# Two rows of gains: folded into scaled rows, or held as columns and applied where turned rows are split

## The chip, the cores and the metric

The kernel runs on one core of a Trainium2 chip. Its time is device microseconds for one execution; several executions give a median. Engines are named as the profile names them: PE (matrix multiplication, and transposition through the same array), DVE (vector), ACT (scalar activations), POOL, and SP, whose only work here is to issue transfers.

## What is computed

Two blocks of a sequence model on 256 tokens of width 2048, all in float32. The part that matters here is the middle of the second block: the residual `x` is normalised once for keys and values, and once for queries, with two different rows of gains (2048 numbers each).

```python
def rmsnorm(x, g):
    xf = x.astype(jnp.float32)
    inv = lax.rsqrt(jnp.mean(xf * xf, axis=-1, keepdims=True) + RMS_EPS)
    return (xf * inv).astype(x.dtype) * g
...
            x = x + (y * jax.nn.silu(gate)) @ w_out_a[i]
            if layer == N_A_LAYERS - 1:
                kv_in = rmsnorm(x, norm_kv)
                k_shared = apply_rope((kv_in @ w_k).reshape(b, s, HEADS_PER_GROUP, HEAD_DIM), cos, sin)
                v_shared = (kv_in @ w_v).reshape(b, s, HEADS_PER_GROUP, HEAD_DIM)
        else:
            i = layer - N_A_LAYERS
            hdn = rmsnorm(x, norm_b[i])
            proj = hdn @ w_in_b[i]
```

Nothing changes `x` between the two normalisations, so both use the same inverse root of the mean square, and only the gains differ.

## The kernel before

Every matrix product is done with three products of rounded parts: a weight tile is split into a high part (ACT, line 852) and the rest, the low part (DVE, line 1275), and activations likewise (`x_high` on ACT, line 879; `x_low` on DVE, line 1299). Weights flow through in units of 0.5 MB (128 partitions x 1024 numbers) in one fixed order: SP loads unit n into one of 4 raw slots once the low part of unit n-4 is made; the split parts sit in 8 slots, so ACT makes the high part of unit n+8 only when PE has used unit n. `freed(n)` in the ACT and DVE programs does that step, and before it one step of whatever stands `aside`. Each engine runs its own program in written order; semaphores tie them together.

The tokens are two halves of 128. A `wide` job computes a 256x512 piece of a product, with 16 tiles of 128 rows of weights, in 8 units of two tiles; for each unit it does half 0, then half 1, three 128x512 matmuls a tile. `wide_by_half` does half 0 over all 8 units and then half 1, so that the rows of half 0 are complete early. The order around the change is: the last pair of gate and group jobs of the pooling layer, four wide jobs `proj_a` (w_out_a; they add to the residual, line 1675), four wide jobs `vals` (w_v), the keys (w_k), then queries with attention.

A row of activations has to be turned (transposed) before it can be the operand that carries the contraction over partitions. `turned` in the PE program (line 652) turns 128x128 tiles against an identity matrix into PSUM (`aux_banks`, 4 banks of 512 columns, so one piece of 4 tiles to a bank, 4 pieces to a half); ACT and DVE then split a piece into `act_a` (keys and values) or `act_b` (queries). DVE first makes the scaled rows, with `rstd` (one number for a token) and the row of gains in one operation (`scale_rows`, line 1315, for keys; line 1709 for queries). The gains are loaded by `load_row` as one row repeated over all partitions, 1 MB each, after the weight units up to the third unit of the second projection job.

## Time and profile before

| | |
|---|---|
| median of 3 runs | 2030.54 us (2030.03 to 2031.4) |
| the profiled execution's own time | 2030.97 us |
| its span, first to last instruction | 2028.8 us |
| PE busy | 2005.8 us (99%) |
| DVE, ACT busy | 1408.6 us (69%), 1010.2 us (50%) |
| mean granted clock | 0.999 |

The span is what the rows below are read against; 2.2 us of the execution lie outside of it. Busy time of PE is the union of its matmuls, so 99% says that it hardly ever stood still, and not how well each matmul was used.

### The profile page before, as it was taken

How to read it: one execution, taken by the hardware profiler on the slowest of the kernel's cores; microseconds unless marked ns; L12 is line 12 of the kernel's file. 1: busy time of each engine (PE TensorE's matmuls, PEld its weight loads, DVE VectorE, ACT ScalarE, POOL GpSimd, SP SyncE). 2: the span in 40 equal slices, each digit the busy share in tenths (PEclk: the TensorE clock that was granted, in tenths of full speed). 3: DMA queues.
4: the chain of work that ended last, by engine and by line, in shares of the span. 5: the costliest groups of instructions: out<-in, count | busy, mean ns of one | idle time of the engine just before them, and what ended most of it. 6: DMA issues, size and time to landing. Idle time of an engine off the chain costs nothing.

```text
span 2028.8 us, 28149 instructions
## 1 busy us (share of the span) xinstructions
PE 2005.8 (99%) x11404; PEld 1759.0 (87%) x11404; DVE 1408.6 (69%) x1722; ACT 1010.2 (50%) x1340; POOL 8.0 (0%) x19
## 2 busy tenths in 40 slices
PE   7999999999999999999999999999999999999998
PEld 7999988888888888888888898888888888888887
DVE  6999967665555555565577766566577888888764
ACT  5767555544444444444455455445444545454543
POOL 0000000000000000000000000000000000000000
PEclk9999999999999999999999999999999999999999
DMA  8655564866656566665637665656565454545573
GB/s 272 187 181 171 182 223 133 275 218 187 196 184 199 186 190 197 186 198 187 195 96 230 188 215 193 227 187 214 187 193 182 151 171 150 173 154 178 171 264 105
DMA packets 305857, 384.24 MB, mean 189 GB/s; under 512 B 11673, under 2 KB 237209, under 8 KB 303936
## 3 DMA queue, kind: packets, MB, share of 16 engines
q1 hardware_dynamic: 305584, 382.38, 59.6%
q8 instruction: 90, 1.47, 0.3%
q14 instruction: 39, 0.32, 0.0%
q10 hardware_dynamic: 144, 0.07, 0.0%
HBM read 378.20 MB, written 4.19 MB: 188 GB/s over the span
## 4 chain that ended last, share of the span: by engine, by line
PE 96%; DMA 1%; DVE 1%; issue 1%; ACT 1%; SPq 0%; POOL 0%; ACTq 0%; POOLq 0%; DVEq 0%
PE job_banks L545 32%; PE job_banks L548 16%; PE job_banks L617 11%; PE job_banks L615 11%; PE job_banks L616 11%; PE job_banks L517 3%; PE job_banks L516 3%; PE job_banks L518 3%; PE aux_banks L787 2%; DMA raw_weights<-in_w_up 1%; PE aux_banks L652 1%; DMA resid<-in_x 1%; PE aux_banks L518 0%; PE aux_banks L517 0%; PE aux_banks L516 0%
## 5 line engine op out<-in xcount | busy, mean ns | idle before, releaser
L1275 DVE TENSOR_TENSOR weights_low<-raw_weights,weights_high 128x1024 fp32r<-128x1024 f32 x696 | 841.8, 1223 | 473.9 <-ACT weights_high L852 468.8
L852 ACT ACTIVATE weights_high<-raw_weights 128x1024 fp32r<-128x1024 f32 x696 | 728.0, 1056 | 605.8 <-PE job_banks L617 243.2
L545 PE MATMUL job_banks<-act_a,weights_high 128*128 128x512 f32 (+1 forms) x2008 | 590.3, 380 | 5.9 <-DVE act_a L1299 4.5
L548 PEld LDWEIGHTS job_banks<-act_a,weights_low 128*128 128x128 f32 x1880 | 347.5, 188 | 75.6
L548 PE MATMUL job_banks<-act_a,weights_low 128*128 128x256 f32 (+1 forms) x1880 | 368.7, 277 | 0.0
L545 PE MATMUL job_banks<-act_b,weights_high 128*128 128x512 f32 x1024 | 326.9, 400 | 0.0
L545 PEld LDWEIGHTS job_banks<-act_a,weights_high 128*128 128x128 f32 x2008 | 303.7, 190 | 7.5 <-issue 5.0
L615 PE MATMUL job_banks<-weights_high,act_b 128*128 128x512 f32 x736 | 287.1, 390 | 0.0
L617 PE MATMUL job_banks<-weights_high,act_b 128*128 128x512 f32 x736 | 286.4, 389 | 0.0
L616 PE MATMUL job_banks<-weights_low,act_b 128*128 128x512 f32 x736 | 286.4, 389 | 0.0
L548 PEld LDWEIGHTS job_banks<-act_b,weights_low 128*128 128x128 f32 x1024 | 192.3, 188 | 45.1
L548 PE MATMUL job_banks<-act_b,weights_low 128*128 128x256 f32 x1024 | 201.5, 278 | 0.0
L516 PE MATMUL job_banks<-act_a,weights_high 128*128 128x256 f32 x576 | 163.2, 283 | 0.0
L617 PEld LDWEIGHTS job_banks<-weights_high,act_b 128*128 128x128 f32 x736 | 138.1, 188 | 28.7
L517 PE MATMUL job_banks<-act_a,weights_high 128*128 128x256 f32 x576 | 163.0, 283 | 0.0
L518 PE MATMUL job_banks<-act_a,weights_low 128*128 128x256 f32 x576 | 163.0, 283 | 0.0
L615 PEld LDWEIGHTS job_banks<-weights_high,act_b 128*128 128x128 f32 x736 | 138.2, 188 | 28.2
L616 PEld LDWEIGHTS job_banks<-weights_low,act_b 128*128 128x128 f32 x736 | 138.2, 188 | 28.2
L545 PEld LDWEIGHTS job_banks<-act_b,weights_high 128*128 128x128 f32 x1024 | 157.2, 189 | 0.8
L517 PEld LDWEIGHTS job_banks<-act_a,weights_high 128*128 128x128 f32 x576 | 110.6, 192 | 0.0
L516 PEld LDWEIGHTS job_banks<-act_a,weights_high 128*128 128x128 f32 x576 | 110.6, 192 | 0.0
L518 PEld LDWEIGHTS job_banks<-act_a,weights_low 128*128 128x128 f32 x576 | 110.6, 192 | 0.0
(146 smaller groups left out, 1683.3 us busy)
## 6 DMA issues: line engine op xcount, KB each, us to landing
raw_weights<-in_w_up SPq DMA_DIRECT2D x128, 512.0 KB, 3.8
raw_weights<-in_w_down SPq DMA_DIRECT2D x128, 512.0 KB, 4.3
raw_weights<-in_w_in_b SPq DMA_DIRECT2D x128, 512.0 KB, 4.1
raw_weights<-in_w_in SPq DMA_DIRECT2D x80, 512.0 KB, 3.9
raw_weights<-in_w_in_a SPq DMA_DIRECT2D x64, 512.0 KB, 4.7
raw_weights<-in_w_out SPq DMA_DIRECT2D x32, 512.0 KB, 4.4
raw_weights<-in_w_out_a SPq DMA_DIRECT2D x32, 512.0 KB, 4.4
raw_weights<-in_w_v SPq DMA_DIRECT2D x32, 512.0 KB, 4.4
```

The source lines that it names most:

```text
L516: e.matmul(o[:, f, :], wh[:, k, cols], xh, start=kt == 0 and f == 0, stop=False)
L517: e.matmul(o[:, f, :], wh[:, k, cols], xl, start=False, stop=False)
L518: made = e.matmul(o[:, f, :], wl[:, k, cols], xh, start=False, stop=kt == job.tiles - 1 and f == 1)
L545: made = e.matmul(o_both, wh[:, k, f * P:(f + 1) * P], rhs, start=opens, stop=False)
L548: made = e.matmul(o[:, 0, low_toks], wl[:, k, f * P:(f + 1) * P], x[:, first + kt, 0, low_toks], start=False, stop=kt == job.tiles - 1)
L615: e.matmul(o, xh, wh[:, k, :], start=opens and kt == 0, stop=False)
L616: e.matmul(o, xh, wl[:, k, :], start=False, stop=False)
L617: made = e.matmul(o, xl, wh[:, k, :], start=False, stop=closes and kt == job.tiles - 1)
L652: made = e.transpose(aux[:, c, i * P:(i + 1) * P], n[:, k * P:(k + 1) * P], ident[:, :])
L787: made = e.matmul(scores_of(half)[:, g, :], q[:, g, half * P:(half + 1) * P], key_t[:, head, 0:(half + 1) * P], start=True, stop=True)
L852: e.activation(high[:, s, :], raw[:, r, :], ACT.Copy).then_inc(*high_done.inc(n))
L1275: e.tensor_tensor(low[:, s, :], raw[:, r, :], high[:, s, :].bitcast(F32), ALU.subtract).then_inc(*low_done.inc(n))
```

## The change

Rows are scaled with `rstd` alone and turned once, for keys. The turned tiles stay in their PSUM bank until both splits have read them: the split for keys multiplies by the gains of `norm_kv`, the split for queries by those of `norm_b`. In the turned layout a gain is one number for a partition, so each of the 16 tiles of 128 columns has its own column of gains, and a piece is split with four operations of 128x128 on ACT and four on DVE instead of one of 128x512 on each. The gains arrive as 16 rows of 128 numbers a vector (8 KB instead of 1 MB), are turned by one PE transpose of 32 rows, and are copied by ACT into a small table (`gain_columns`), which takes the place of other early tables. The second half's rows can be turned into a bank only when the queries' split of the first half has read it; the turns of half 1 are therefore spread over the first `vals` job, behind its units given by `TURNS_OF_KEYS`, instead of standing in one block between its halves.

```diff
+TURNS_OF_KEYS = ((0, 4), (0, 7), (1, 0), (1, 1))
...
 (sync)
             e.wait_ge(*x_low.at(("pooled", N_POOL - 1)))
-            load_row(0, "norm_kv", t["norm_kv_2"])
-            load_row(1, "norm_b", t["norm_b_2"][0])
+            for i, src in enumerate((t["norm_kv_2"], t["norm_b_2"][0])):
+                e.dma_start(gain_rows[i * KT:(i + 1) * KT, :], src.rearrange("(a n) -> a n", a=KT)).then_inc(
+                    *gains_ready.inc("gains", by=16))
...
 (tensor)
+            e.wait_ge(*gains_ready.at("gains"))
+            e.transpose(aux[:, 0, 0:2 * KT], gain_rows, ident[0:2 * KT, 0:2 * KT]).then_inc(*gains_turned.inc("gains"))
             for job in proj_a[:-1]:
                 wide(job, "b", gated_comes)
+            e.wait_ge(*gains_kept.at("gains"))
             wide_by_half(proj_a[-1:], "b", gated_comes, 0, lambda: turned("keys", 0, 3, 1, ("pool", 1)))
             aside.finish()
-            def second_keys():
-                run_all(turned("keys", 1, 0, before=("keys", 0)))
-                yield
-
-            wide_by_half(vals[0:1], "a", by_four("keys"), 0, second_keys)
-            aside.finish()
-            aside.begin(turned("queries", 0, 3, 2, ("keys", 1)))
-            aside.begin(turned("queries", 1, 1, 2, ("queries", 0)))
+
+            turns = turned("keys", 1, 1, 1, ("queries", 0))
+            next(turns)
+            for half in range(HALVES):
+                for u in range(vals[0].count):
+                    made = wide_unit(vals[0], "a", 0, u, half, True, True, by_four("keys"))
...
+                    if (half, u) in TURNS_OF_KEYS:
+                        next(turns)
...
 (scalar)
+            def split_gained(name, half, c, buf, first):
+                for k in range(4 * c, 4 * c + 4):
+                    made = e.activation(parts_of_x(buf, slice(k, k + 1), (half,))[0], turned_tile(k), ACT.Copy,
+                                        scale=gain_columns[:, first + k:first + k + 1])
+                made.then_inc(*x_high.inc((name, half, c)))
...
+            e.wait_ge(*gains_turned.at("gains"))
+            e.activation(gain_columns, aux[:, 0, 0:2 * KT], ACT.Copy).then_inc(*gains_kept.inc("gains"))
+            e.wait_ge(*gains_kept.at("gains"))
...
 (vector)
+            def scale_keys(half):
+                e.wait_ge(*rstd_made.at(("keys", half)))
+                for c, cols in enumerate(PIECES):
+                    e.tensor_scalar(wide_rows[:, half, cols], resid[:, half, cols], rstd[:, half:half + 1], None,
+                                    ALU.mult).then_inc(*row_scaled.inc(("keys", half, c)))
...
             take_added(proj_a[-1], 3, 1)
-            aside.finish()
+            freed(proj_a[-1].last - 2)
+            mean_squares("keys", 1, ("x_a", 3, 1))
+            split_queries(0, 0)
+            scale_keys(1)
+            freed(proj_a[-1].last - 1)
+            freed(proj_a[-1].last)
+            split_queries(0, 1)
+            split_keys(1, 0)
+            split_queries(0, 2)
+            split_keys(1, 1)
+            split_queries(0, 3)
+            split_keys(1, 2)
+            split_keys(1, 3)
...
-            def norm_queries(half, pause):
-                h, n = resid[:, half, :], wide_rows[:, half, :]
-                e.wait_ge(*rows_turned.at(("keys", half, 3)))
-                e.wait_ge(*row_ready[1].at("norm_b"))
-                for c, cols in enumerate(PIECES):
-                    e.scalar_tensor_tensor(n[:, cols], h[:, cols], rstd[:, half:half + 1], rows[1][:, cols],
-                                           ALU.mult, ALU.mult).then_inc(*row_scaled.inc(("queries", half, c)))
-                yield from turned("queries", half, "b", pause, 2)
```

The first place is PE's program where the last group job (lines 516 to 518, their numbers before) hands over to the first projection job (lines 615 to 617). In brackets stand the semaphores that an instruction waits for. Before:

```order
L516 MATMUL aux_banks<-act_b,weights_high 128x256
L517 MATMUL aux_banks<-act_b,weights_high 128x256
L518 MATMUL aux_banks<-act_b,weights_low 128x256
L615 MATMUL job_banks<-weights_high,act_b 128x512 [waits x_low,low_done,gathered]
L616 MATMUL job_banks<-weights_low,act_b 128x512
```

And in the changed kernel, whose lines lie 10 further on:

```order
L526 MATMUL aux_banks<-act_b,weights_high 128x256
L527 MATMUL aux_banks<-act_b,weights_high 128x256
L528 MATMUL aux_banks<-act_b,weights_low 128x256
L764 MATMUL aux_banks<-ident,scratch 128x32 [waits gains_ready]
L625 MATMUL job_banks<-weights_high,act_b 128x512 [waits x_low,low_done,gathered]
L626 MATMUL job_banks<-weights_low,act_b 128x512
```

One instruction is new, the transpose of the 32 rows of gains, and it waits for `gains_ready`, which the two small transfers raise. It stands ahead of the whole projection.

The second place is the queue of SP, which feeds that wait. In the changed kernel:

```order
L431 DMA raw_weights<-in_w_in_a 128x4x256 [waits low_done] x4
L431 DMA raw_weights<-in_w_grp_a 128x4x256 [waits low_done] x2
L431 DMA raw_weights<-in_w_out_a 128x2x512 [waits low_done] x11
L473 DMA scratch<-in_norm_kv 16x128 [waits x_low]
L473 DMA scratch<-in_norm_b 16x128
L431 DMA raw_weights<-in_w_out_a 128x2x512 [waits low_done] x21
```

Only the shape of the two loads differs from before (there 128x2048 each): they still stand behind 11 units of w_out_a, each of which waits for a low part.

The third place is DVE's program from the end of the last projection job into the first `vals` job: `resid<-resid,job_banks` is the last addition to the residual of half 1, `weights_low` a low part, `early_tables` the columns of gains. Before:

```order
L1275 TENSOR_TENSOR weights_low<-raw_weights,weights_high 128x1024 [waits high_done] x4
L1675 TENSOR_TENSOR resid<-resid,job_banks 128x512 [waits unit_used]
L1307 TENSOR_REDUCE sumsq<-sumsq 128x1 [waits consts_made,squared,const_ready]
L1315 SCALAR_TENSOR_TENSOR wide_rows<-resid,rstd,scratch 128x512 [waits row_ready0,rstd_made]
L1315 SCALAR_TENSOR_TENSOR wide_rows<-resid,rstd,scratch 128x512 x3
L1299 TENSOR_TENSOR act_a<-aux_banks,act_a 128x4x128 [waits x_high] x4
L1275 TENSOR_TENSOR weights_low<-raw_weights,weights_high 128x1024 [waits high_done] x8
```

And in the changed kernel:

```order
L1327 TENSOR_TENSOR weights_low<-raw_weights,weights_high 128x1024 [waits high_done]
L1727 TENSOR_TENSOR resid<-resid,job_banks 128x512 [waits unit_used]
L1327 TENSOR_TENSOR weights_low<-raw_weights,weights_high 128x1024 [waits high_done]
L1359 TENSOR_REDUCE sumsq<-sumsq 128x1 [waits consts_made,squared]
L1734 SCALAR_TENSOR_TENSOR act_b<-aux_banks,early_tables,act_b 128x128 [waits gains_kept,x_high]
L1734 SCALAR_TENSOR_TENSOR act_b<-aux_banks,early_tables,act_b 128x128 x3
L1747 TENSOR_SCALAR wide_rows<-resid,rstd 128x512 [waits rstd_made]
L1747 TENSOR_SCALAR wide_rows<-resid,rstd 128x512 x3
L1327 TENSOR_TENSOR weights_low<-raw_weights,weights_high 128x1024 [waits high_done] x2
L1734 SCALAR_TENSOR_TENSOR act_b<-aux_banks,early_tables,act_b 128x128 [waits gains_kept,x_high]
L1734 SCALAR_TENSOR_TENSOR act_b<-aux_banks,early_tables,act_b 128x128 x3
L1734 SCALAR_TENSOR_TENSOR act_a<-aux_banks,early_tables,act_a 128x128 [waits gains_kept,x_high]
```

The last addition, which had stood behind the last three low parts of the `vals` job's first eight units, moves ahead of them; between them now stand a split for queries and the scaling, and ahead of the following low parts stand seven splits of four operations each.

## Rows read from the trace of the kernel before

**Rows 1.** First part of the page: busy us (share of the span) xinstructions

```profile
PE 2005.8 (99%) x11404; PEld 1759.0 (87%) x11404; DVE 1408.6 (69%) x1722; ACT 1010.2 (50%) x1340; POOL 8.0 (0%) x19
```

**Rows 2.** Waits of PE over the whole span: total us, times, longest

```profile
PE job_banks L615 <- DVE act_a L1299: 0.2, 1, 0.2
```

**Rows 3.** Timeline, PE: first matmul of the projection behind the last group job

```profile
1259.39 0.40 PE L615 MATMUL job_banks<-weights_high,act_b 128*128 128x512 f32 x1
```

**Rows 4.** Timeline, queue of SP (start us, issue us)

```profile
1261.38 0.37 SPq L422 DMA_DIRECT2D raw_weights<-in_w_out_a  x1
1261.79 0.47 SPq L429 DMA_DIRECT2D scratch<-in_norm_kv  x1
1262.30 0.43 SPq L429 DMA_DIRECT2D scratch<-in_norm_b  x1
```

**Rows 5.** DMA issues by tile: count, KB each, median us to landing

```profile
raw_weights<-in_w_out_a SPq DMA_DIRECT2D x32, 512.0 KB, 4.4
...
out<-wide_rows SPq DMA_DIRECT2D x8, 256.0 KB, 2.5
...
scratch<-in_norm_kv SPq DMA_DIRECT2D x1, 1024.0 KB, 6.6
```

**Rows 6.** Windows: busy us of five engines, granted clock, DMA share, GB/s

```profile
1261.50:1262.25 0.75, 0.75 (x5) 0.63 (x4) 0.75 (x2) 0.00 (x0) 0.00 (x0) 1.00 0.00 0
1262.25:1265.25 3.00, 3.00 (x15) 2.49 (x14) 1.87 (x3) 1.53 (x2) 0.00 (x0) 1.00 0.74 220
```

**Rows 7.** Timeline, PE: idle time ahead of a matmul in brackets

```profile
1057.00 1.86 PE L545 MATMUL job_banks<-act_a,weights_high 128*128 128x256 f32 x8 [2.14 <-DVE act_a L1299]
```

**Rows 8.** Windows behind that idle time, columns as in rows 6

```profile
1057.20:1060.60 3.40, 3.40 (x17) 3.30 (x17) 3.34 (x6) 0.60 (x1) 0.55 (x1) 0.50 0.03 7
1060.60:1064.00 3.40, 3.40 (x31) 3.40 (x30) 3.40 (x5) 1.69 (x3) 0.00 (x0) 1.00 0.11 23
```

**Rows 9.** Timeline, PE: last matmul before and third behind each block of transposes

```profile
1339.43 0.40 PE L617 MATMUL job_banks<-weights_high,act_b 128*128 128x512 f32 x1
...
1340.57 0.40 PE L617 MATMUL job_banks<-weights_high,act_b 128*128 128x512 f32 x1
...
1358.32 0.39 PE L617 MATMUL job_banks<-weights_high,act_a 128*128 128x512 f32 x1
...
1358.99 0.39 PE L617 MATMUL job_banks<-weights_high,act_a 128*128 128x512 f32 x1
...
1361.87 0.39 PE L617 MATMUL job_banks<-weights_high,act_a 128*128 128x512 f32 x1
...
1380.23 0.40 PE L617 MATMUL job_banks<-weights_high,act_a 128*128 128x512 f32 x1
...
1381.80 0.40 PE L617 MATMUL job_banks<-weights_high,act_a 128*128 128x512 f32 x1
```

**Rows 10.** Groups by shape, DVE: count, busy us, mean ns, idle before

```profile
L1275 DVE TENSOR_TENSOR weights_low<-raw_weights,weights_high 128x1024 fp32r<-128x1024 f32 x696 | 841.8, 1223 | 473.9 <-ACT weights_high L852 468.8
...
L1755 DVE TENSOR_TENSOR scratch<-scratch 128x256 f32<-128x256 f32 x32 | 13.3, 414 | 0.6
...
L1755 DVE TENSOR_TENSOR scratch<-scratch 128x128 f32<-128x128 f32 x32 | 9.1, 283 | 0.6
...
L1458 DVE SCALAR_TENSOR_TENSOR scratch<-scratch,early_tables 128x256 f32<-128x256 f32 x16 | 6.7, 478 | 0.0
...
L1817 DVE TENSOR_SCALAR wide_rows<-wide_rows,rstd 128x512 f32<-128x512 f32 x4 | 1.8, 483 | 1.3 <-POOL rstd L1842 1.3
```

**Rows 11.** Groups by shape, ACT

```profile
L852 ACT ACTIVATE weights_high<-raw_weights 128x1024 fp32r<-128x1024 f32 x696 | 728.0, 1056 | 605.8 <-PE job_banks L617 243.2 <-PE job_banks L548 231.6 <-PE job_banks L518 36.9
...
L1196 ACT ACTIVATE scratch<-scratch,soft 128x128 f32<-128x128 f32 x16 | 6.2, 388 | 0.0
```

**Rows 12.** Timeline, all engines: key scaling of half 0, first matmul of the values

```profile
1338.14 2.74 DVE L1315 SCALAR_TENSOR_TENSOR wide_rows<-resid,rstd,scratch 128x512 f32<-128x512 f32 x4 [0.73 <-POOL rstd L1842]
...
1348.34 0.39 PE L615 MATMUL job_banks<-weights_high,act_a 128*128 128x512 f32 x1
```

More of the change, by code:

```diff
@@ L324, in build @@
         staging = scratch[0:ROWS, D:D + D_A]
+        gain_rows = scratch[0:2 * KT, 0:P]
         gpad_n = TOKENS + CONV_B - 1
@@ L359, in weights_of, with turned_tile @@
             return e_flat[:, lo:lo + (half + 1) * GROUPS * P].rearrange("p (g n) -> p g n", g=GROUPS)
+        def turned_tile(k):
+            return aux[:, k // 4:k // 4 + 1, k % 4 * P:(k % 4 + 1) * P]
         def column(row, j):
@@ L1148, in scalar @@
             take_added("x_a", 3, 0)
-            aside.begin(turned("keys", 0, "a", 2, 1, pool_gate[-1].last))
-            units_of(proj_a[-1])
-            take_added("x_a", 3, 1)
-            aside.finish()
-            run_all(turned("keys", 1, "a", 0))
+            aside.begin(first_keys())
+            e.wait_ge(*unit_used.at(pool_gate[-1].last))
+            for n in range(proj_a[-1].at, proj_a[-1].last - 2):
+                freed(n)
+            aside.finish()
+            e.wait_ge(*unit_used.at(("half", proj_a[-1].id)))
+            split_queries(0, 0)
+            freed(proj_a[-1].last - 2)
+            take_added("x_a", 3, 1)
+            split_queries(0, 1)
[4 more added lines that the diff above has]
+            split_queries(0, 3)
+            for c in range(1, len(PIECES)):
+                split_keys(1, c)
             def keep_vals(c):
@@ L1159, in keep_vals @@
                     if c == 0:
-                        e.wait_ge(*rows_turned.at(("queries", half, 3)))
+                        e.wait_ge(*rows_turned.at(("keys", half, 3)))
                     e.activation(wide_rows[:, half, PIECES[c]], banks[:, 2 * job.pair + half, :],
@@ L1164, in scalar @@
             units_of(vals[0])
-            for half in range(HALVES):
-                aside.begin(turned("queries", half, "b", 1 if half else 3, 2, proj_a[-1].last))
             for n in range(vals[1].at, vals[1].last + 1):
                 freed(n)
+                if n < vals[1].at + 4:
+                    split_queries(1, n - vals[1].at)
                 if n == vals[1].at + 5:
-                    aside.finish()
                     keep_vals(0)
@@ L1675, in take_added, with split_gained, split_keys, split_queries @@
                 e.tensor_tensor(h, h, banks[:, 2 * job.pair + half, :], ALU.add).then_inc(*taken.inc((job.id, half)))
-            def norm_keys(half, pause):
-                mean_squares("keys", half, ("x_a", 3, half))
-                if half == 0:
-                    e.wait_ge(*x_low.at(("grp", N_POOL - 1)))
-                scale_rows("keys", half, 0, "norm_kv")
-                yield from turned("keys", half, "a", pause)
+            def split_gained(name, half, c, buf, first):
+                e.wait_ge(*x_high.at((name, half, c)))
+                e.wait_ge(*gains_kept.at("gains"))
+                for k in range(4 * c, 4 * c + 4):
+                    hi, lo = parts_of_x(buf, slice(k, k + 1), (half,))
+                    made = e.scalar_tensor_tensor(lo, turned_tile(k), gain_columns[:, first + k:first + k + 1],
+                                                  hi.bitcast(F32), ALU.mult, ALU.subtract)
+                made.then_inc(*x_low.inc((name, half, c)))
+            def split_keys(half, c):
+                split_gained("keys", half, c, "a", 0)
+            def split_queries(half, c):
+                split_gained("queries", half, c, "b", KT)
+            def scale_keys(half):
[3 more added lines that the diff above has]
+                                    ALU.mult).then_inc(*row_scaled.inc(("keys", half, c)))
+            def first_keys():
+                mean_squares("keys", 0, ("x_a", 3, 0))
+                e.wait_ge(*x_low.at(("grp", N_POOL - 1)))
+                scale_keys(0)
+                yield
+                yield
+                for c in range(len(PIECES)):
+                    split_keys(0, c)
+                    yield
             for c, job in enumerate(proj_a[:-1]):
```

49 lines of the change are left out of this document (39 added, 10 removed).

## The prediction

> **What bounds the kernel now.** I read the page first: PE is busy for 2005.8 us, 99% of the span [rows 1]. So only two kinds of thing count: instructions that PE no longer has to execute or has to in addition, and time in which PE stands still. The waits of PE say where it stood still before; around this change that is a single 0.2 us, for the low part of the first keys' piece of half 1 (`act_a`, line 1299) [rows 2]. From the last group job through the `vals` jobs PE therefore runs back to back, and DVE and ACT matter only when they make it wait. The next views are timelines of PE, SP and DVE at the two places at which PE gets new waits: the start of the projection (1259.39 us) [rows 3] and the first `vals` job (1348.34 us) [rows 12].
>
> **What the change takes off PE.** Rows were turned four times 16 tiles, and will be turned twice 16. The price of a block is what it adds between two third-part matmuls (line 617) that lie three matmuls apart, which is 0.68 us where nothing stands between (1358.99 - 1358.32 to the hundredth, 0.227 us for one) [rows 9]. A block of four costs 1340.57 - 1339.43 - 0.68 = 0.46 us, a block of 16 costs 1361.87 - 1358.99 - 0.68 = 2.20 us (with the 0.2 us wait), and a block of eight costs 1381.80 - 1380.23 - 0.68 = 0.89 us [rows 9]. Gone are the block of 16 and the four blocks of eight for queries: 2.20 + 4 x 0.89 = 5.76 us. New are four blocks of four in the first `vals` job: 4 x 0.46 = 1.84 us. Net: 3.9 us less. The four blocks for half 0 of the keys stay as they are.
>
> **The wait for the gains.** PE's new transpose stands ahead of the projection and waits for both small transfers. In the trace PE issues the projection's first matmul at 1259.39 us [rows 3], but SP issues the two gain loads only at 1261.79 and 1262.30, directly behind a weight unit issued at 1261.38, which had waited for a low part [rows 4]. Before, that lateness cost nothing: the gains were first read at 1338.14 [rows 12]. That was 70 us of slack behind their landing; now it is a deficit. Nothing on SP's side gets earlier by the change, since the same 11 units stand ahead of the loads. PE stands still from 1259.39 to their landing.
>
> When do they land? The row of a small load in this place does not exist. From below: the smallest median landing in the trace is 2.5 us (256 KB of output) [rows 5], giving 1262.30 + 2.5 = 1264.8. From above: the 1 MB load of gains in the same place landed 6.6 us after its issue, 1268.4 [rows 5]. In between: the weight unit of 1261.38 lies ahead in the same queue, and w_out_a units land after 4.4 us in the median, 1265.8 [rows 5]; the DMA engines move nothing from 1261.5 to 1262.25, and 220 GB/s x 3.0 us = 0.66 MB until 1265.25, which is that unit's 0.52 MB and the start of the gains [rows 6]. 16 KB behind it add almost nothing, so I take 1265.7, near the row of the unit that they follow. The Trainium skill ("DMA: Bandwidth & Descriptors", section "Anatomy of one DMA — SWDGE (gpsimd) path") gives a fixed cost of about 2 us to a transfer, most of it the receipt of its last bytes; an estimate by that page alone, with nothing ahead in the queue, would be 1264.3 and a sum 1.4 us smaller, and no row here shows a transfer that short.
>
> The wait is thus 1265.7 - 1259.39 = 6.3 us (5.4 to 9.0). The transpose itself and the restart of the weight pipeline are priced by the nearest row, a whole block of four transposes, 0.46 us; I take 0.4. Behind PE nothing has to be caught up: ACT and DVE are eight units ahead when it stands still and stay so, and no later wait of PE exists that could absorb the shift. Sum of this step: +6.7 us (5.8 to 9.4).
>
> **The clock behind it.** The granted clock is 1.00 (2.4 GHz) nearly everywhere. After PE's idle 2.14 us in front of 1057.00 [rows 7] it stands at 0.50 (1.2 GHz) from 1057.2 to 1060.6, with 17 matmuls in 3.40 us, against 31 in the next 3.40 us at 1.00 [rows 8]. A gap three times that long should bring it down too. If 3.4 us of the projection run at half the rate, 3.4 / 2 = 1.7 us are lost. Below it is nothing (if the clock stays, or is low only while PE stands still), above 3.4 us (two such stretches). I take 1.7.
>
> **The first `vals` job.** DVE and ACT are given more work in the stretch where they feed PE most closely. Prices: a DVE operation of 128x128 takes 283 ns, one of 128x256 with a column operand 478 instead of 414 ns [rows 10], so 283 + 64 = 347 ns for one with a column, about 1.1 us for four that overlap a little; on ACT the nearest row is 388 ns for 128x128 with a column, from SBUF [rows 11], about 1.2 us for four. Scaling of a half gets cheaper, four of at most 483 ns [rows 10], about 1.7 us as they overlap, instead of 2.74 [rows 12].
>
> I let DVE's new program run with these from 1338.14, low parts at 1.2 us each [rows 10] and ACT's high parts at 1.06 [rows 11]. The low part of unit 4 is done at 1350.9, the residual addition at 1351.6, low part 5 at 1352.8, queries' split (0,0) at 1354.2, the scaling of half 1 at 1355.9, low parts 6 and 7 at 1357.1 and 1358.3. PE needs unit 6 at 1348.34 + 6 x 1.36 + 0.46 = 1357.0 and unit 7 at 1358.3: right at the edge, 0 to 0.4 us late. Then follow queries (0,1) at 1359.5, in front of the turn behind (0,7) at 1359.8; keys (1,0) at 1360.7, wanted at 1360.3 (0.4 late); queries (0,3) at 1364.1, in front of the last turn at 1363.9 (0.2 late). Everything behind has over 2 us. I take 1.0 us of waits in all; from below 0, and from above 3, if four operations in a row do not overlap (0.15 to 0.4 us more for each of about eight pieces ahead of PE's need). What waits behind DVE there is `low_done` for PE and, through the raw slots, the next weight loads; they have 7 us of slack.
>
> The queries' splits of half 1 lie beside the second `vals` job, 1.2 us of DVE work added to 1.2 a unit, under the 2.72 us that PE takes for one. The two scalings for queries (8 operations on DVE) and 2 MB of loads go, under PE, at nothing; were that cover gone, the operations alone would be 5.4 us.
>
> **Sum.** -3.9 + 6.7 + 1.7 + 1.0 = +5.5 us. The profiled execution took 2030.97 us, 2.2 more than its span and 0.4 more than the median, 2030.54. On its own time that gives 2036.5, on the median **2036.0 us**.
>
> **The rivals.**
> *The gains' wait is hidden* (the other side: not slower). If both land before PE gets to 1259.39, only the turns and the waits in `vals` stay: -3.9 + 1.0 = -2.9 us, 2027.6. It decides where the wait is shorter than 2.9 us, that is a landing before 1262.3, when the second load is only being issued [rows 4]. For it speaks only that other executions might issue earlier; against it that SP's queue hangs on the low parts, which hang on PE. Chance 0.05.
> *A short wait, and the clock stays up.* Landing at 1264.8, transposes in passing: -3.9 + 5.8 + 0 + 1.0 = +2.9 us, 2033.4. For it: 2.5 us rows exist [rows 5]; against it: the load ahead in the queue, and the fall of the clock after 2.14 us [rows 8]. Chance 0.12.
> *DVE becomes the bound in the first `vals` job.* With the upper prices, or with a weight unit landing late there, units 6 and 7 and each of the four turns hold PE: +5 instead of +1, 2040.0. For it: margins of under half a microsecond; against it: the scaling has become cheaper. Chance 0.08.
>
> **How the numbers follow.** The forecast has 0.75. Its own bounds reach from -3.9 + 5.8 + 0.4 + 0 = +2.3 to about +9; the second rival lies inside the lower edge, the third around the upper. From 2033.0 to 2039.5 leaves out the hidden wait and half of each edge. A measurement of this kernel tells about 0.2% from no change, 4.1 us. Faster by more than that: 0.03 (a hidden wait and no waits in `vals`). Within it: the rest of the first rival, the second and 0.07 of the forecast, 0.22. Slower: 0.75.
>
> **What would show it.** In the profile of the changed kernel: the waits of PE hold one of 5 to 9 us in front of the 128x32 transpose, put down to a DMA of `scratch<-in_norm_b`; the windows show a granted clock of 0.50 for some 3 us behind it; PE has 32 transposes of 128x128 fewer (128 at that line); three or four waits under 0.6 us each for `act_b`, `act_a` or low parts in the first `vals` job. The prediction is wrong if the gains are issued much earlier than 2.4 us behind PE's need, if they pass the load ahead of them, or if the small operations cost much less or more than the rows of their neighbours say.

## The result, and the profile after

| | before | changed |
|---|---|---|
| median of 10 runs each, same chip | 2030.78 us | 2036.01 us |
| lowest, highest | 2029.84, 2032.1 | 2034.34, 2036.64 |
| ratio of the times | | 1.0024, 95% interval 1.0015 to 1.0033 |
| profiled execution, its span | 2030.97, 2028.8 | 2034.44, 2032.6 |

The change made the kernel 5.2 us slower on the medians, where +5.5 was predicted. Two executions, one of experiment 2 (2846.32 us) and one of the kernel before beside experiments 9 and 10 (2851.59 us), had a mean granted clock of 0.655 and are in no ratio and no profile below. The page of the changed kernel, against [rows 1]:

```profile
PE 2004.2 (99%) x11373; PEld 1756.5 (86%) x11373; DVE 1407.8 (69%) x1762; ACT 1017.5 (50%) x1389; POOL 8.0 (0%) x19
```

PE executes 31 instructions fewer (32 turns gone, one new), DVE has 40 operations more, 48 for 8 less, and no more busy time; and yet the end is later. So the loss isn't in busy time, and the waits of PE come next (engine, tile and line, what it waited for: total us, times, longest), against [rows 2]:

```profile
PE aux_banks L764 <- DMA scratch<-in_norm_b: 5.9, 1, 5.9
...
PE aux_banks L662 <- DVE act_b L1734: 0.3, 1, 0.3
```

The first is the wait for the gains at the projection's start. The second is all that the first `vals` job waits. How the first comes about is in the timeline of SP's queue (start us, issue us), against [rows 4]:

```profile
1255.31 5.51 SPq L431 DMA_DIRECT2D raw_weights<-in_w_out_a  x2
1260.86 0.46 SPq L473 DMA_DIRECT2D scratch<-in_norm_kv  x1
1261.37 0.42 SPq L473 DMA_DIRECT2D scratch<-in_norm_b  x1
```

and in the view of landings (count, KB, median us from issue to landing), against [rows 5]:

```profile
scratch<-in_norm_kv SPq DMA_DIRECT2D x1, 8.0 KB, 3.3
scratch<-in_norm_b SPq DMA_DIRECT2D x1, 8.0 KB, 3.1
```

The last of the two weight units is issued at 1260.45 us, directly ahead of the gains. In the view of landings for 1260 to 1262 us alone it is this row:

```profile
raw_weights<-in_w_out_a SPq DMA_DIRECT2D x1, 512.0 KB, 3.6
```

So the unit lands at 1264.05 us and the second load of gains 0.4 us behind it. Then PE's timeline, against [rows 3]; the last number in a row is the idle time ahead of it:

```profile
1258.34 0.28 PE L528 MATMUL aux_banks<-act_b,weights_low 128*128 128x256 f32 x1
1264.49 0.31 PE L764 MATMUL aux_banks<-ident,scratch 32*128 32x32 f32 x1 [5.87 <-DMA scratch<-in_norm_b]
1264.73 0.80 PE L625 MATMUL job_banks<-weights_high,act_b 128*128 128x512 f32 x1
...
1267.88 0.63 PE L626 MATMUL job_banks<-weights_low,act_b 128*128 128x512 f32 x1
1268.31 0.43 PE L627 MATMUL job_banks<-weights_high,act_b 128*128 128x512 f32 x1
1268.58 0.39 PE L625 MATMUL job_banks<-weights_high,act_b 128*128 128x512 f32 x1
```

PE reaches the transpose at 1258.6 us; the second load, issued at 1261.37, lands 3.1 us later, so PE stands for 5.87 us. Behind it the matmuls start every 0.43 us up to 1268.31, and every 0.23 us from 1268.58 on. From 1264.73 to 1268.58 there are nine, in 3.85 us; at full clock, nine take 2.04: 1.8 us lost. The windows (busy us of five engines, granted clock, DMA share, GB/s) say why, against [rows 8]:

```profile
1259.00:1261.00 2.00, 0.00 (x0) 0.00 (x0) 1.81 (x3) 1.10 (x2) 0.00 (x0) 1.00 0.05 17
1261.00:1263.00 2.00, 0.00 (x0) 0.00 (x0) 1.75 (x3) 0.21 (x1) 0.00 (x0) 0.64 0.56 171
1263.00:1265.00 2.00, 0.51 (x2) 0.45 (x3) 1.12 (x1) 1.01 (x2) 0.00 (x0) 0.50 0.72 202
1265.00:1267.00 2.00, 2.00 (x5) 1.55 (x6) 0.10 (x1) 0.03 (x1) 0.00 (x0) 0.50 0.41 160
1267.00:1269.00 2.00, 2.00 (x7) 1.59 (x6) 0.00 (x0) 0.00 (x0) 0.00 (x0) 0.65 0.00 0
1269.00:1271.00 2.00, 2.00 (x10) 1.63 (x9) 0.35 (x1) 1.06 (x1) 0.00 (x0) 1.00 0.00 0
```

The granted clock falls to 0.50 (1.2 GHz) while PE is still idle, stays there for some 6.8 us, and PE runs the projection in the last 3.7 of them.

The small operations, in DVE's timeline and against [rows 10] and [rows 12]: scaling without the gains, a split with columns for keys, then, last, the low parts of units 6 and 7, for which PE was to wait:

```profile
1345.29 1.68 DVE L1747 TENSOR_SCALAR wide_rows<-resid,rstd 128x512 f32<-128x512 f32 x4 [0.73 <-POOL rstd L1923]
...
1348.62 1.13 DVE L1734 SCALAR_TENSOR_TENSOR act_a<-aux_banks,early_tables,act_a 128x128 fp32r<-128x128 f32 x4 [0.52 <-ACT act_a L1163]
1349.66 1.22 DVE L1327 TENSOR_TENSOR weights_low<-raw_weights,weights_high 128x1024 fp32r<-128x1024 f32 x1
1350.79 1.12 DVE L1734 SCALAR_TENSOR_TENSOR act_a<-aux_banks,early_tables,act_a 128x128 fp32r<-128x128 f32 x4
...
1361.71 2.35 DVE L1327 TENSOR_TENSOR weights_low<-raw_weights,weights_high 128x1024 fp32r<-128x1024 f32 x2
```

Where the shift arises, in the two profiled executions (changed less before; at the projection, where the changed kernel would start without the wait):

| point on PE | before | changed | difference | what lies between |
|---|---|---|---|---|
| projection | 1259.39 | 1258.46 | -0.93 | nothing of the change |
| first matmul of `vals` | 1348.34 | 1355.50 | +7.16 | +8.09: wait 5.87, transpose and restart 0.4, clock 1.82 |
| first matmul of the keys | 1441.22 | 1444.92 | +3.70 | -3.46: turns and waits in `vals` |
| end of the span | 2028.8 | 2032.6 | +3.8 | nothing |

The -0.93 is not the change's, for nothing of the change lies ahead of this point on PE. At the matmul behind the gap near 344 us the changed kernel is 0.38 us ahead (344.37 against 344.75), at the one near 1057 us 1.34 (1055.66 against 1057.00). In between only the kernel before has this wait of 0.71 us in its trace, which is most of the difference:

```profile
389.69 0.70 PE L545 MATMUL job_banks<-act_a,weights_high 128*128 128x512 f32 x2 [0.71 <-DVE value L1292]
```

Behind 1057 us, where the clock fell at another moment in each, the changed kernel loses 0.4 us of it again. The window over the stretch of `vals` in the kernel before:

```profile
1348.34:1441.22 92.88, 92.68 (x433) 77.14 (x432) 58.08 (x61) 45.68 (x54) 0.55 (x1) 1.00 0.68 224
```

The same stretch in the changed kernel, with 31 matmul records fewer:

```profile
1355.50:1444.92 89.42, 89.12 (x402) 73.56 (x400) 57.48 (x92) 51.34 (x90) 0.55 (x1) 1.00 0.70 231
```

### The profile page after: what moved, and what is told of

It reads as the page before. It is cut to its first block, busy times and chain, and to the rows that moved or that the text cites. A ratio compares the mean times of both kernels' runs of the same rounds, so it can differ in the third digit from the quotient of the medians.

```text
span 2032.6 us, 28187 instructions
## 1 busy us (share of the span) xinstructions
PE 2004.2 (99%) x11373; PEld 1756.5 (86%) x11373; DVE 1407.8 (69%) x1762; ACT 1017.5 (50%) x1389; POOL 8.0 (0%) x19
## 4 chain that ended last, share of the span: by engine, by line
PE 97%; issue 1%; DMA 1%; ACT 1%; DVE 1%; SPq 0%; POOL 0%; ACTq 0%; POOLq 0%; DVEq 0%
PE job_banks L555 33%; PE job_banks L558 16%; PE job_banks L625 11%; PE job_banks L627 11%; PE job_banks L626 11%; PE job_banks L527 3%; PE job_banks L526 3%; PE job_banks L528 3%; PE aux_banks L804 2%; PE aux_banks L662 1%; DMA resid<-in_x 1%; PE aux_banks L627 0%; PE aux_banks L625 0%; PE aux_banks L626 0%; PE aux_banks L822 0%
## 5 line engine op out<-in xcount | busy, mean ns | idle before, releaser
L869 ACT ACTIVATE weights_high<-raw_weights 128x1024 fp32r<-128x1024 f32 x696 | 727.8, 1057 | 609.8 <-PE job_banks L627 251.7
```

The source lines that it names most:

```text
L869: e.activation(high[:, s, :], raw[:, r, :], ACT.Copy).then_inc(*high_done.inc(n))
```

## The experiments

Theory: the change is worth some -3.5 us on its own (turns off PE), and the place of the two small loads costs some +8 (wait, restart, clock). The rival for the loss is DVE and ACT in the first `vals` job. Each kernel was compared with runs of the kernel before on the same chip.

**1. The gains issued earlier.** The order of SP's queue alone is changed.

```diff
 (sync)
-            through(grp[-1][-1])
+            through(pool_gate[3])
             e.wait_ge(*x_low.at(("pooled", N_POOL - 1)))
...
+            through(grp[-1][-1])
             through(proj_a[-1])
```

> The changed kernel with one thing moved: SP issues the two small gain loads right behind the weight units of the fourth gate job, some 60 us before PE wants them. Wait theory (PE stands 5.9 us for the gains and then runs about 3.7 us at half clock): both go, the savings of the turns stay. Against before: -3.9 for the turns, +0.5 for waits in the first vals job, +0.1 for the small transpose, so about -3.3 us, ratio 0.9984. Rival (the small splits or the spread turns cost the time, and the wait is absorbed elsewhere): still 3 to 5 us slower than before, ratio 1.002.

Measured: 2028.44 against 2031.65 us, ratio 0.9983 (0.9974 to 0.9992). The waits of PE hold no row for the gains any more; 0.3 us for `act_b` stay. The change without this wait is faster than before by 3.2 us, though a load here takes 5.1 and 5.8 us to land: it is waited for by nobody.

**2. The gains turned later.** The loads stay where they are; PE's wait and transpose, and ACT's copy with its two waits (not shown), move behind the first projection job.

```diff
 (tensor)
-            e.wait_ge(*gains_ready.at("gains"))
-            e.transpose(aux[:, 0, 0:2 * KT], gain_rows, ident[0:2 * KT, 0:2 * KT]).then_inc(*gains_turned.inc("gains"))
             for job in proj_a[:-1]:
                 wide(job, "b", gated_comes)
+                if job is proj_a[0]:
+                    e.wait_ge(*gains_ready.at("gains"))
+                    e.transpose(aux[:, 0, 0:2 * KT], gain_rows, ident[0:2 * KT, 0:2 * KT]).then_inc(
+                        *gains_turned.inc("gains"))
...
```

> The changed kernel with the loads left where they are, and the wait, the transpose and ACT's copy moved behind the first projection job, 21.8 us later. Wait theory: the loads have landed by then, so the same as with the earlier loads, about -3.3 us against before, ratio 0.9984. Rival (it is not the lateness but something about the small loads, for example that they take over 20 us): a wait remains. Rival (splits and turns cost it): 3 to 5 us slower than before.

Measured: 2028.53 us, ratio 0.9983 (0.9974 to 0.9992). PE's timeline at the new place:

```profile
1280.37 0.39 PE L627 MATMUL job_banks<-weights_high,act_b 128*128 128x512 f32 x1
1280.68 0.24 PE L767 MATMUL aux_banks<-ident,scratch 32*128 32x32 f32 x1
1280.86 0.49 PE L625 MATMUL job_banks<-weights_high,act_b 128*128 128x512 f32 x1
```

No idle time, and 0.49 - 0.23 = 0.26 us from start to start beyond a matmul. Both cures give the same time from opposite ends (the loads earlier, the need later), so the place of the loads as against the need is the cause, and not the loads' size or the transpose.

**3. The gap filled.** PE turns the identity 44 times into a bank that nobody reads, ahead of its wait. The gains come no earlier; only PE has something to do.

```diff
 (tensor)
+            for _ in range(44):
+                e.transpose(aux[:, 1, 0:P], ident[:, :], ident[:, :])
             e.wait_ge(*gains_ready.at("gains"))
```

> The changed kernel with 44 transposes of the identity matrix into an unused bank put ahead of the wait, about 5.1 us of work for PE inside of the 5.9 us in which it stood still; their results are used by nobody. Clock theory (1.8 us of the loss in the profiled run, up to 3.4 in others, is the half clock behind the wait): the wait of PE falls to under 1.5 us, the granted clock stays at 1.00, and the kernel gains 1.8 to 2.7 us on the changed kernel: +3 us against before, ratio 1.0013. Rival (the clock costs nothing that the wait does not already cover): as the changed kernel, +5.2 us, ratio 1.0026.

Measured: 2033.70 us, ratio 1.0011 (1.0002 to 1.002), +2.05 us. Three consecutive windows around the remaining wait of 1.0 us:

```profile
1262.00:1264.00 2.00, 2.00 (x21) 2.00 (x20) 2.00 (x4) 0.00 (x0) 0.00 (x0) 1.00 0.33 54
1264.00:1266.00 2.00, 1.23 (x12) 0.99 (x10) 0.88 (x2) 1.06 (x1) 0.00 (x0) 1.00 0.75 253
1266.00:1268.00 2.00, 1.75 (x8) 1.46 (x9) 0.91 (x1) 0.20 (x1) 0.00 (x0) 1.00 0.72 232
```

The clock stays at 1.00 (2.4 GHz). The time until the gains land is lost as before, and what was gained against the changed kernel is the clock's share: 5.2 - 2.05 = 3.2 us, where 1.8 were to be had. The intervals of the two (some 1.8 us to either side each) cover the difference. The size of 1.8 is read from rows; this run shows that work in the gap keeps the clock up, and that this saves time.

**4. The wait alone.** The kernel before gets the small loads, the wait, the transpose and ACT's copy, and no other part of the change; its two 1 MB loads come behind.

```diff
 (sync)
+            for i, src in enumerate((t["norm_kv_2"], t["norm_b_2"][0])):
+                e.dma_start(gain_rows[i * KT:(i + 1) * KT, :], src.rearrange("(a n) -> a n", a=KT)).then_inc(
+                    *gains_ready.inc("gains", by=16))
+            e.wait_ge(*gains_turned.at("gains"))
             load_row(0, "norm_kv", t["norm_kv_2"])
 (tensor)
+            e.wait_ge(*gains_ready.at("gains"))
+            e.transpose(aux[:, 0, 0:2 * KT], gain_rows, ident[0:2 * KT, 0:2 * KT]).then_inc(*gains_turned.inc("gains"))
             for job in proj_a[:-1]:
```

> The kernel before with one part of the change alone: the two small gain loads at their place in the queue, the transpose of them ahead of the projection and ACT's copy. The columns are read by nobody, the 1 MB loads follow behind the transpose, all scaling, turning and splitting is as before. Wait theory: 6.3 us for wait and restart and 1.8 to 2.7 us for the clock, so +8 to +9 us against before, ratio 1.0042. Rival (the wait is short by itself and only the change's other parts make it cost): under +4 us.

Measured: 2040.06 us, ratio 1.0041 (1.0028 to 1.0053), +8.4 us. Its waits of PE:

```profile
PE aux_banks L763 <- DMA scratch<-in_norm_b: 5.9, 1, 5.9
```

The window over the stretch at a granted clock of 0.50:

```profile
1262.87:1269.70 6.83, 3.21 (x8) 2.57 (x9) 3.07 (x4) 1.25 (x2) 0.00 (x0) 0.50 0.54 174
```

The same 5.9 us as in the changed kernel, and the clock at 0.50 for 6.8 us. The loss is there without any of the change's work on DVE and ACT: that rival is out as its cause. Experiments 1 and 4 also add up: -3.2 + 8.4 = +5.2 us, what the change measured.

**5. One unit earlier.** The gains go ahead of the last weight unit that they had followed, with nothing in between.

```diff
 (sync)
-            through(grp[-1][-1])
+            loads(grp[-1][-1].last + SPLIT_SLOTS + RAW_SLOTS - 2)
...
+            through(grp[-1][-1])
             through(proj_a[-1])
```

> The changed kernel with the two gain loads one weight unit earlier in SP's queue: behind 10 units of w_out_a instead of 11. In the changed kernel's profile the tenth unit was issued at 1255.3 and the eleventh only at about 1260.4, since it waited for a low part; the loads would so be issued at about 1255.8 and 1256.2, and land 3 us later, at about 1259.2, against 1258.5 at which PE gets there. Lateness theory: the wait of PE falls from 5.9 to 0.5 to 1.5 us, the clock stays at 1.00, and the kernel is 2 to 2.5 us faster than before, ratio 0.9989. Rival (the landing takes long by itself, whatever stands ahead): a wait of over 3 us and a clock that falls, no faster than before.

Measured: 2031.01 against 2031.42 us, ratio 1.0000 (0.9991 to 1.0009), where 0.9989 was expected: a miss. The timeline of SP's queue:

```profile
1252.71 5.16 SPq L431 DMA_DIRECT2D raw_weights<-in_w_out_a  x4
1257.91 0.46 SPq L473 DMA_DIRECT2D scratch<-in_norm_kv  x1
1258.42 1.47 SPq L473 DMA_DIRECT2D scratch<-in_norm_b  x1
```

PE's timeline at the wait:

```profile
1262.45 0.24 PE L765 MATMUL aux_banks<-ident,scratch 32*128 32x32 f32 x1 [1.64 <-DMA scratch<-in_norm_b]
```

And the window behind it:

```profile
1263.10:1266.50 3.40, 3.40 (x10) 2.61 (x9) 2.28 (x4) 1.14 (x2) 0.00 (x0) 0.50 0.55 170
```

The wait shrank to 1.64 us, just over the 0.5 to 1.5 expected, for the second load landed 4.0 us after its issue instead of 3. And behind this gap too the clock fell in the profiled execution, for 3.4 us and with PE at work in all of them. I had expected it to stay. Eight matmuls at 0.43 us instead of 0.23 are 1.6 us lost: -3.5 + 1.6 + 0.4 + 1.6 = +0.1 us, where -0.4 was measured on the medians.

**6. Ahead of its unit, at the same time.** As 5, but the gains wait for the low part for which that unit waits. They are thus issued when the changed kernel issues them, with no unit directly ahead in the queue.

```diff
+            loads(grp[-1][-1].last + SPLIT_SLOTS + RAW_SLOTS - 2)
+            e.wait_ge(*low_done.at(grp[-1][-1].last + SPLIT_SLOTS - 1))
```

> The changed kernel with the two gain loads ahead of the eleventh unit of w_out_a, but held by the same low part as that unit: they are issued 0.4 us earlier than in the changed kernel, at about 1260.4 and 1260.9, and no weight unit is in the queue in front of them. My prediction took the unit ahead for most of the landing time. If so, the second load lands 2.0 to 2.5 us after its issue instead of 3.0, the wait is 4.7 us instead of 5.9, and the kernel is 1.2 us faster than the changed one: +4 us against before, ratio 1.0020. If what stands ahead makes no difference, only the 0.4 us of the issue are gained, and the wait is 5.4 us: +4.8 us, ratio 1.0024.

Measured: 2034.81 against 2031.42 us, ratio 1.0017 (1.0008 to 1.0026), +3.4 us; the wait is 4.69 us, against 5.87. The timeline of SP's queue:

```profile
1261.05 0.42 SPq L474 DMA_DIRECT2D scratch<-in_norm_b  x1
```

The landings:

```profile
scratch<-in_norm_kv SPq DMA_DIRECT2D x1, 8.0 KB, 1.7
scratch<-in_norm_b SPq DMA_DIRECT2D x1, 8.0 KB, 2.4
```

With no weight unit directly ahead, the second load lands after 2.4 us; with one 0.5 MB unit just ahead after 3.1 (changed kernel); behind four units issued in 5.2 us after 4.0 (experiment 5). The unit ahead was worth 0.7 us, where the prediction took it for most of the landing time. The Trainium skill ("DMA: Bandwidth & Descriptors", section "Anatomy of one DMA — SWDGE (gpsimd) path") has a fixed cost of about 2 us for a transfer issued from POOL. The two loads of this run, which SP issues, took 1.7 and 2.4 us, near it.

The window over the stretch at 0.50:

```profile
1261.63:1268.46 6.83, 4.93 (x12) 3.90 (x13) 2.57 (x3) 1.14 (x2) 0.00 (x0) 0.50 0.50 156
```

The stretch is as long as in the changed kernel and starts at the same place (1261.63 us, against 1261.57), but PE is at work for 4.9 us of it: eleven matmuls from 1263.77 to 1268.55 us take 4.78 us instead of 2.5, so 2.3 us are lost instead of 1.8. Of the 1.2 us taken off the wait, the clock takes back 0.5. The parts, -3.5 + 4.7 + 0.4 + 2.3 = +3.9 us, lie within the interval of the +3.4 measured.

**7. The turns of half 1 in one block.** As 2, with the four turns together behind unit 7, as in the kernel before. This asks what the queries' splits, which have to free the banks, cost if they are not spread.

```diff
-TURNS_OF_KEYS = ((0, 4), (0, 7), (1, 0), (1, 1))
+TURNS_OF_KEYS = ((0, 7),)
...
-                        next(turns)
+                        run_all(turns)
```

> The kernel with the gains turned behind the first projection job, and the four turns of half 1 in one block between the halves of the first vals job, as before the change, instead of spread. The last two turns must wait until DVE has split queries (0,2) and (0,3), and the split of queries (0,3) stands in DVE's program behind that of keys (1,1). From the changed kernel's profile, queries (0,3) is done 1.5 us behind the split of keys (1,1), which is 2.2 us behind its turn: PE waits about 2.7 us before the last turn instead of 0.3, so 2.4 us more than with the spread turns, and up to 1.8 us more if the clock falls behind it. Against before: -0.9 to +0.9 us, ratio 1.0000. Rival (the spread is not needed, a block has all that it needs): -3.3 us, ratio 0.9983.

Measured: 2034.20 us, ratio 1.0016 (1.0007 to 1.0025), where 1.0000 was expected, a miss: 5.7 us above experiment 2. The timeline of PE:

```profile
1358.90 1.03 PE L662 MATMUL aux_banks<-ident,wide_rows 128*128 128x128 f32 x8
1363.02 0.63 PE L662 MATMUL aux_banks<-ident,wide_rows 128*128 128x128 f32 x4 [3.08 <-DVE act_b L1737]
1365.08 1.09 PE L662 MATMUL aux_banks<-ident,wide_rows 128*128 128x128 f32 x4 [1.44 <-DVE act_b L1737]
```

The timeline of DVE:

```profile
1360.71 1.13 DVE L1737 SCALAR_TENSOR_TENSOR act_a<-aux_banks,early_tables,act_a 128x128 fp32r<-128x128 f32 x4 [3.09 <-ACT act_a L1165]
1361.75 1.12 DVE L1737 SCALAR_TENSOR_TENSOR act_b<-aux_banks,early_tables,act_b 128x128 fp32r<-128x128 f32 x4
```

My estimate had DVE free its banks one after the other from the start. But its program puts the keys' split (1,0) ahead of the queries' (0,2), and that split needs PE's first turn, which now comes late: DVE stood still for 3.09 us, and PE waited 3.08 and 1.44 us for what was queued behind. The waits are 4.2 us longer than the 0.3 of experiment 2, and in the trace the clock is at 0.50 from 1363.81 to 1370.64, 5.6 us of it with PE at work, 2.8 lost. Behind the start of `vals` (1348.02 us here, 1348.17 there) the spans, 2032.1 and 2025.3 us, differ by 7.0 us, which is the two together. With DVE's program in this order, spreading the turns is therefore what keeps the wait in this job at 0.3 us. A block with an order of splits made for it was not run.

**8. The old gaps filled, at a wrong place.** Experiment 3 suggested filling the two older gaps, near 344 and 1057 us, where PE waits 2.05 and 2.14 us for the low part of `act_a` behind the first units of a pair of jobs [rows 7]. As 2, with 16 matmuls of zeros, which add nothing to their bank, ahead of the second pass of such a pair. The expectation for this run takes it that the clock falls behind the second gap always; in the profile of experiment 4 it had stayed up there.

```diff
                 run_all(turns)
+                for _ in range(16):
+                    e.matmul(o[:, :, 0:P], zeros[:, :], act_a[:, 0, :, 0:P], start=False, stop=False)
                 second_pass(two, "a", by_four(name), soon + last)
```

> The kernel with the gains turned behind the first projection job, and 16 matmuls with a tile of zeros (256 columns each, added to a bank that is being summed, so they change no value) in the two older gaps of PE, of 2.05 us near 345 us and 2.14 us near 1057 us, behind which the granted clock is at 0.50 for 3.4 us in the second always and in the first in some executions. Clock theory: the gaps are busy, the clock stays at 1.00 at both places, and 1.6 us are gained in every execution and 1.6 more in some, so 1.6 to 3 us on the same kernel without them: -5 to -6 us against before, ratio 0.9973. Rival (the fall of the clock costs nothing there, since other engines bound those stretches): as without them, ratio 0.9983, or slower by what the zeros take beyond the gap.

Measured: 2031.09 us, ratio 0.9995 (0.9986 to 1.0004), 2.6 us above experiment 2 (4.2 on the spans, 2029.5 against 2025.3). PE's timeline shows a miss of placement:

```profile
344.55 3.04 PE L556 MATMUL job_banks<-act_a,weights_high 128*128 128x256 f32 x16 [2.05 <-DVE act_a L1359]
...
350.72 2.15 PE L612 MATMUL job_banks<-act_a,zeros 128*128 128x256 f32 x16
```

The gap lies ahead of the fourth unit of the first pass. The zeros come 6.2 us behind its end here and 4.6 us at the other place, took 2.15 us each time and filled nothing.

**9. The old gaps filled, in place.**

```diff
             def first_pass(two, buf, comes, order):
-                for i in order:
+                for n, i in enumerate(order):
+                    if n == 3:
+                        e.wait_ge(*consts_made.at("zeros"))
+                        o = banks[:, 2 * two[0].pair, :].rearrange("p (a n) -> p a n", a=2)
+                        for _ in range(15):
+                            e.matmul(o[:, :, 0:P], zeros[:, :], act_a[:, 0, :, 0:P], start=False, stop=False)
```

> The kernel with the gains turned behind the first projection job, and 15 matmuls with a tile of zeros (256 columns each, about 1.9 us, added to a bank that is being summed, so they change no value) behind the third unit of each first pass, which is where PE stands still for 2.05 us near 344 us and 2.14 us near 1057 us; the run before had them some 8 us too late, in stretches in which PE was busy. Clock theory: the two idle times shrink to under 0.4 us, the granted clock stays at 1.00 at both places, and 1.6 us are gained in every execution and 1.6 more in those in which the first gap also brought the clock down: 1.6 to 3 us on the same kernel without zeros, so -5 to -6 us against before, ratio 0.9973, and less scatter between executions. Rival (the half clock there costs nothing, because DVE and ACT bound those stretches anyway, or the zeros only take the gap's place): ratio 0.9983.

Measured: 2025.81 against 2030.46 us, ratio 0.9974 (0.9964 to 0.9984): the fastest of all, 4.65 us below the kernel before, where 5 to 6 were expected. PE's timeline at both places:

```profile
342.25 1.96 PE L594 MATMUL job_banks<-act_a,zeros 128*128 128x256 f32 x15
344.45 1.78 PE L556 MATMUL job_banks<-act_a,weights_high 128*128 128x256 f32 x13 [0.25 <-DVE act_a L1360]
...
1055.75 1.19 PE L556 MATMUL job_banks<-act_a,weights_high 128*128 128x256 f32 x8 [0.34 <-DVE act_a L1360]
```

Three windows that follow one another:

```profile
345.00:349.00 4.00, 4.00 (x37) 4.00 (x36) 3.93 (x7) 1.60 (x4) 0.28 (x1) 1.00 0.00 0
349.00:1057.00 708.00, 707.60 (x3650) 603.85 (x3648) 426.71 (x439) 318.99 (x365) 2.19 (x4) 1.00 0.62 193
1057.00:1062.00 5.00, 4.57 (x38) 4.33 (x39) 5.00 (x8) 2.29 (x4) 0.00 (x0) 1.00 0.01 2
```

The real matmuls start no earlier for the zeros (344.45 against 344.47 us in experiment 2); what is won is the clock behind them. Seven of the eight runs lie between 2025.78 and 2025.9 us, where those of the kernel before spread over 2 us. The rival's ratio of 0.9983 still lies inside of the interval, at its edge. Against it speak the single runs: these seven lie 0.6 us or more below every run of experiments 1, 2 and 10 (the lowest is 2026.5, in experiment 10, on the same chip).

**10. The splits in one operation.** As 2, with one 128x512 operation for a split on ACT and on DVE, which leaves the gains out. Shown is ACT; DVE's four become one subtraction.

```diff
-                for k in range(4 * c, 4 * c + 4):
-                    made = e.activation(parts_of_x(buf, slice(k, k + 1), (half,))[0], turned_tile(k), ACT.Copy,
-                                        scale=gain_columns[:, first + k:first + k + 1])
+                made = e.activation(parts_of_x(buf, four(c), (half,))[0],
+                                    aux[:, c, :].rearrange("p (k n) -> p k n", n=P), ACT.Copy)
```

> The kernel with the gains turned behind the first projection job, and each split of a turned piece done with one operation of 128x512 on ACT and one on DVE instead of four of 128x128 on each; the gains of keys, values and queries are left out of the computation. My prediction gave 1.0 us of waits of PE in the first vals job to the four-part splits; the changed kernel's profile shows 0.3 us, before the last turn. If the small splits are what makes it late, that wait is gone and the stretch of the vals jobs is 0.4 us shorter: ratio against before 0.9981, not to be told from 0.9983 by time, but by the waits of PE. Rival (the wait comes from the order of the splits on DVE, not from their size): it stays at 0.3 us.

Measured: 2028.28 against 2030.46 us, ratio 0.9984 (0.9974 to 0.9993), no different from experiment 2. The 0.3 us wait for `act_b` is gone; `vals` takes 88.94 us (1349.81 to 1438.75) instead of 89.44 (1348.17 to 1437.61). By these two traces the four-fold operations cost PE 0.5 us.

## Why the prediction was right

**Turns off PE (-3.9) and waits in the first `vals` job (+1.0).** Together -2.9 predicted; the stretch of `vals` shortened by 3.46 us, and the change free of the gains' wait measured -3.2 and -3.1 (experiments 1 and 2). The operations were priced well: a split with columns takes 1.12 us on DVE (1.1), the scaling of a half 1.68 (1.7), one such operation on DVE 342 ns (347). The term for waits was mis-sized: 0.3 us instead of 1.0. I had lined up full durations, where the trace's steps from start to start are 0.08 to 0.09 us shorter: a split starts at 1348.62 and the next work at 1349.66, 1.04 us later, and a low part at 1349.66 is followed at 1350.79, after 1.13. By my count of eight low parts and some six splits up to PE's need this makes about 1.2 us, an estimate: low parts 6 and 7 were done at 1364.06, where my schedule, moved by the 7.15 us of the scaling's start, gives 1365.45.

**The wait for the gains (+6.7).** Measured 5.87 + 0.4 = 6.3. SP issued its loads 0.9 us earlier than before, as PE did the projection, since the low parts hang on PE: the distance of 2.9 us between PE's need and the second issue was the same (1262.30 - 1259.39, 1261.37 - 1258.46). The landing, 3.4 us assumed, took 3.1. The step took it from the weight unit ahead, which was to land after 4.4 us; it landed after 3.6, and the gains 0.4 us behind it, so the rule that they land with that unit held. As a cause it was too strong: with the unit behind instead of ahead the load still took 2.4 us, and 0.7 us is what the unit was worth (experiment 6).

**The clock behind it (+1.7).** Measured 1.8. The step said that the clock stays low for 3.4 us with PE at work; in fact it was low for 6.8 us, and 3.1 of them lay ahead of the projection's first matmul. The size came out right with half of the stretch unforeseen, which is partly luck. The price doesn't grow with the wait: 1.6 us were lost behind 1.64 us of waiting in experiment 5, 2.3 behind 4.69 in experiment 6, 1.8 behind 5.87 in the changed kernel, and 2.8 behind 3.08 and 1.44 in experiment 7.

**Sum.** In the profiled executions: 8.09 - 3.46 - 0.93 = +3.7 on the spans (3.8), and without the 0.93, which isn't the change's, +4.6. The medians say +5.2, the lowest runs of each 2034.34 - 2029.84 = +4.5. Part of the spread is probably how often the clock fell elsewhere (last section). The edges were added up wrongly: -3.9 + 5.8 + 0.4 + 0 counts the 0.4 of the transpose twice, since 5.8 holds it, and the upper bounds make -3.9 + 9.4 + 3.4 + 3.0 = +11.9, not about +9. Its own bounds thus reach from +1.9 to +11.9, wider than the range of +2.5 to +9; the measured +5.2 lies well inside of both.

**The rivals.** Gains hidden: not so in the changed kernel, and worth -3.2 and -3.1 us against before where it was made so (-2.9 forecast; experiments 1 and 2). Short wait with the clock up: experiment 6 had a landing as short as this rival's and a wait of 4.69 us, experiment 5 one of 1.64 us, and the clock fell in both. DVE as the bound: not so, with 0.3 us of waits; a wait of PE for DVE's splits of over a microsecond came only where the turns stand in a block (experiment 7).

## What to carry to other kernels

When a load's first reader moves, compare the time of its issue with the new need, and not the amount of data: 8 KB in place of 1 MB did not save PE from standing still, for the queue issued it 2.9 us behind the need. Put the step that waits where the queue has long delivered, or the load ahead of units that hang on the waiting engine. Where PE is 99% busy, count its gaps twice, once as idle time and once for the clock behind them: shortening a gap can move more work under the low clock (experiment 6), and a gap that can't be closed may be filled with matmuls of zeros, at the place that the timeline shows. And line up a chain of operations by their steps from start to start, not by their durations.

## What the runs showed of the hardware

- Behind a gap of PE of 1.64 us (experiment 5) and behind gaps of 2.05 and 2.14 us the granted clock was at 0.50 for about 3.4 us. With gaps of 4.69 and 5.87 us it was so for 6.8 us, the start of which lay in the gap. Behind gaps of 1.21 us (near 391.65 us in experiment 5), 1.02 us (experiment 3), 0.49 and 0.34 us (experiment 9) it stayed up. A 2 us gap is followed by the low clock in some executions only: near 344 us the clock fell in the profiles of experiments 1, 3, 4, 5, 8 and 10 and stayed up in those of both kernels and of 2, 6 and 7; near 1057 us it stayed up in 4, 5, 7 and 8. Why in these executions is open. The 1.64 us gap was seen in one profile alone, so how often the clock falls behind it isn't known either.
- The two old gaps are the most likely source of the 2 us over which the executions of one kernel spread: with both filled, seven of eight runs agree within 0.12 us. Another may be the wait near 390 us, 0.7 to 1.2 us long, which the traces of the kernel before and of experiments 4, 5 and 7 have and the others don't. One run at 2027.2 remains unexplained.
- At 0.50 a 128x512 matmul starts every 0.43 us instead of 0.23.
